# Attention without mask matmuls and with half-tile output work, and shorter lookups in the expert ranking, in a one-core encoder layer

## The reference

```python
s = einsum('bqhd,bkhd->bhqk', qb, k) * DA_DK ** -0.5       # 2 streams of 8 heads, 64 wide
mask = kchunk[None, :] <= (qpos // CHUNK)[:, None]         # chunks of 64 tokens
p = softmax(where(mask, s, -inf)).reshape(b, 8, 2, nq, nk)
a = p[:, :, 0] - lam * p[:, :, 1]
o = einsum('bhqk,bkhd->bqhd', a, v)                        # then normed per head and merged
...
t1, i1 = top_k(s1, 16); t2, i2 = top_k(s2, 16)             # PEER: per token and head
ts, ci = top_k(t1[:, None] + t2[None, :], 16)              # 16 best of the 256 sums
e = i1[ci // 16] * 128 + i2[ci % 16]                       # look up the two ranks' places
```

## Time and profile before

| | us |
|---|---|
| three runs | 2456.37, 2452.95, 2452.42 (median 2452.95) |
| the profiled execution | 2453.18 |
| its span, first to last instruction | 2451.4 |
| busy in the span: PE, DVE, ACT, POOL | 2297.4, 1542.0, 666.7, 1169.1 |
| attention and ranking within it | about 482 to 727, and about 998 to 1328 |

### The profile page before, as it was taken

How to read it: one execution, slowest core, us unless ns; L and a number is a source line. 1 busy time by engine, 2 the same in 40 slices (tenths; PEclk the granted TensorE clock), 3 DMA queues, 4 the chain that set the end, 5 groups by cost and what they waited for, 6 DMA issues and landing times.

```text
span 2451.4 us, 29790 instructions
## 1 busy us (share of the span) xinstructions
PE 2297.4 (94%) x11005; PEld 1758.7 (72%) x11005; DVE 1542.0 (63%) x2697; ACT 666.7 (27%) x1421; POOL 1169.1 (48%) x744
## 2 busy tenths in 40 slices
PE   6999999989979999998998999999799999999996
PEld 5899977755557987998998999999544444444442
DVE  3376654454553033699999999999455555555555
ACT  2334420133331122233343544444100100001011
POOL 8754555400003404426665777777344544445441
PEclk9999999955679999999999999999899999999998
DMA  6423233210031303226555999999999999999994
GB/s 232 149 95 107 97 106 120 99 47 18 17 116 55 131 30 130 78 89 219 171 176 149 352 355 359 360 370 346 327 359 380 376 386 374 373 382 383 379 382 167
DMA packets 220195, 541.96 MB, mean 221 GB/s; under 512 B 20129, under 2 KB 119266, under 8 KB 211106
## 3 DMA queue, kind: packets, MB, share of 16 engines
q1 hardware_dynamic: 113024, 243.30, 29.3%
q0 software_dynamic: 55424, 201.42, 21.6%
q10 hardware_dynamic: 51618, 95.52, 10.8%
HBM read 472.18 MB, written 67.67 MB: 220 GB/s over the span
## 4 chain that ended last, share of the span: by engine, by line
PE 56%; DVE 31%; issue 5%; DMA 4%; ACT 2%; SPq 2%; POOL 1%; ACTq 0%; POOLq 0%; DVEq 0%
PE ps L975 24%; PE ps L601 17%; DVE ring_u L1903 5%; PE ps L719 5%; DVE ps L1912 3%; PE ps L752 3%; DMA ge<-ge_scratch 3%; DVE hot L2059 2%; DVE hot L2057 2%; PE ps L580 2%; PE ps L802 2%; PE ps L756 1%; SPq L450 1%; DVE pickp L1983 1%; POOL wL L495 1%
## 5 line engine op out<-in xcount | busy, mean ns | idle before, releaser
L975 PE MATMUL ps<-vraw,gf 128*128 128x512 f32 x1536 | 665.7, 596 | 23.6 <-DVE gf L2073 14.5
L975 PEld LDWEIGHTS ps<-vraw,gf 128*128 128x128 f32 x1536 | 293.1, 191 | 395.6 <-issue 373.6
L510 POOL DMA_INDIRECT ring_u<-u_rows,place_of x192 | 234.4, 1221 | 414.2 <-DVE ring_u L1903 393.8
L491 POOL TENSOR_SCALAR wH<-raw 128x1024 fp32r<-128x1024 f32 x112 | 122.6, 1113 | 627.1 <-PE ps L601 475.7
L501 POOL TENSOR_TENSOR uL<-uraw,uH 128x1024 fp32r<-128x1024 f32 x128 | 323.3, 2539 | 116.6 <-ACT uH L1415 115.6
L927 PE MATMUL ps<-actH,uH 128*128 128x384 f32 x1024 | 347.9, 340 | 7.7 <-POOL uL L501 7.0
L927 PE MATMUL ps<-actL,uH 128*128 128x384 f32 x1024 | 343.6, 336 | 0.0
L927 PE MATMUL ps<-actH,uL 128*128 128x384 f32 x1024 | 343.4, 335 | 0.0
L1903 DVE SCALAR_TENSOR_TENSOR ring_u<-ring_u,xn 128x1024 f32<-128x1024 f32 x192 | 312.7, 1629 | 0.0
L601 PE MATMUL ps<-actH,wH 128*128 128x288 f32 (+1 forms) x960 | 287.4, 299 | 9.2 <-DVE actL L1573 9.2
L601 PE MATMUL ps<-actL,wH 128*128 128x288 f32 (+1 forms) x960 | 285.2, 297 | 0.0
(11 more groups left out here) (293 smaller groups left out, 3422.3 us busy)
## 6 DMA issues: line engine op xcount, KB each, us to landing
uraw<-wu SPq DMA_DIRECT2D x128, 512.0 KB, 4.6
vraw<-wv SPq DMA_DIRECT2D x128, 512.0 KB, 7.4
raw<-wts SPq DMA_DIRECT2D x56, 1024.0 KB, 4.9
ge_scratch<-ge ACTq DMA_DIRECT2D x128, 192.0 KB, 4.6
c_scratch<-cst ACTq DMA_DIRECT2D x12, 2048.0 KB, 10.1
cg<-c_scratch SPq DMA_DIRECT2D x32, 768.0 KB, 12.8
ge<-ge_scratch SPq DMA_DIRECT2D x128, 192.0 KB, 8.3
xres<-x ACTq DMA_DIRECT2D x2, 2048.0 KB, 11.9
```

Of the source, the lines that this page charges most:

```text
L491: pool.tensor_scalar(hi[:, cut], w[:, cut], 1.0, 1.0, ALU.mult, ALU.mult).then_inc(high_done, 1)
L510: pool.indirect_dma_start(out=ring_u[:, s % RING, :], out_offset=None, in_=a["u_rows"], in_offset=bass.IndirectOffsetOnAxis(ap=place_of[:, ...
L975: mm = pe.matmul(bank(2 * i + half), gf[:, q % GF_RING, i * P:(i + 1) * P], vraw[:, q % V_RING, half * CHUNK:(half + 1) * CHUNK], start=q ...
```

## The change

- No mask matmuls, no mask tensor and no load of it; each score matmul closes its own group.
- `maxima` takes two reductions, one over the first n-64 keys for all rows and one over the last 64 keys for rows 64 to 127 alone, and then the smaller of the two (negated) results for these rows. `exps` takes two activations per stream, split the same way, each with its own sum; the excluded block of the matrix is set to zero once at the start, and `combine` first adds the two sums (`zb` stays zero in the upper rows).
- In tiles 0 to 3 PE issues `scores` two units ahead, and DVE takes `maxima(u)` ahead of `combine(u-1)`. Tile 4 keeps the old order.
- Outputs are copied, normed, turned and merged by half tile (four heads, one PSUM bank), spread over the following eight units; `merge` is cut into `scale_outputs` and `merge`; the loads come by half tile too.
- In `rank`, the winner at place t of 16 can only have a rank below 4 for t < 4 and below 8 for t < 8, so the three lookups go over 4*4 + 4*8 + 8*16 = 176 instead of 256 elements per head and half, each cut into three instructions.

```diff
-                    mm = pe.matmul(bank(b, n), qT[half, h, t], kT[half, h, 0:n], start=True, stop=False)
+                    mm = pe.matmul(bank(b, n), qT[half, h, t], kT[half, h, 0:n], start=True, stop=True)
-                    mm = pe.matmul(ps[:, b * BANK + n - DK:b * BANK + n], mask[0:1, 0:P], mask[0:1, P:P + DK],
-                                   start=False, stop=True)
...
-            if h == 0 and i > 0:
-                pe.wait_ge(turned_used, i)
+            if h % 4 == 0 and i > 0:
+                pe.wait_ge(turned_used, 2 * i + h // 4 - 1)
...
         scores(0)
+        scores(1)
         for u, (i, h) in enumerate(UNITS):
-            if u + 1 < len(UNITS):
+            if u + 2 < pairs:
+                scores(u + 2)
+            elif pairs <= u + 1 < len(UNITS):
                 scores(u + 1)
             turn_probs(u)
-            if h == 1 and i > 0:
-                turn_outputs(i - 1)
+            if h % 4 == 3 and u > 3:
+                turn_outputs((u - 3) // 4 - 1)
...
+                    act.activation(prob[:, u % 2, s, 0:n - DK], bank(b, n - DK), ACT.Exp,
+                                   bias=sm["nmax"][:, col:col + 1], accum_out=sm["z"][:, col:col + 1])
+                    ins = act.activation(prob[DK:P, u % 2, s, n - DK:n], ps[DK:P, b * BANK + n - DK:b * BANK + n],
+                                         ACT.Exp, bias=sm["nmax"][DK:P, col:col + 1],
+                                         accum_out=sm["zb"][DK:P, col:col + 1])
...
+            j = (u - 4) // 4
+            if j >= 0 and h % 4 == 1:
+                copy_outputs(j)
+            if j >= 0 and h % 4 == 2:
+                root(j)
+            if j >= 1 and h % 4 == 1:
+                merged_high(j - 1)
+            if j >= 2 and h % 4 == 1:
+                act.wait_ge(ml_done, j - 1)
+                load_merge(j)
...
+                ve.tensor_reduce(nmax, src[:, :, 0:n - DK], AX, ALU.max, negate=True)
+                step.done(ve.tensor_reduce(sm["nm"][DK:P, :], src[DK:P, :, n - DK:n], AX, ALU.max, negate=True))
+                ve.tensor_tensor(nmax[DK:P], nmax[DK:P], sm["nm"][DK:P, :], ALU.min).then_inc(nm_ready, 1)
...
+                step.done(ve.tensor_tensor(rz, z, sm["zb"][:, 2 * (u % 2):2 * (u % 2) + 2], ALU.add))
...
+        ve.wait_ge(sc_ready, 1)
+        step.done(ve.memset(sm["zb"], 0.0))
+        for b in range(2):
+            ins = ve.memset(prob[0:DK, b].rearrange("p s (i k) -> p s i k", k=P)[:, :, :, DK:P], 0.0)
         for u, (i, h) in enumerate(UNITS):
-            if u > 0:
+            if i == TILES - 1:
                 combine(u - 1)
             maxima(u)
+            if u > 0 and i < TILES - 1:
+                combine(u - 1)
+            j = (u - 4) // 4
+            if j >= 0 and h % 4 == 2:
+                variance(j)
+            if j >= 0 and h % 4 == 3:
+                scale_outputs(j)
+            if j >= 1 and h % 4 == 0:
+                merge(j - 1)
+            if j >= 1 and h % 4 == 2:
+                merged_low(j - 1)
...
+            parts = [(slice(0, 4), 4), (slice(4, 8), 8), (slice(8, TOPK), TOPK)]
             for half in range(2):
-                step.done(ve.tensor_tensor(flat, ..., ALU.is_equal))
-                step.done(ve.tensor_tensor(hit, hit, ..., ALU.mult))
-                step.done(ve.tensor_reduce(chosen[0:rows, at, half, mine], flat, AX, ALU.add))
+                for ts, w in parts:
+                    ins = ve.tensor_tensor(hit[:, :, ts, 0:w], ..., ALU.is_equal)
+                step.done(ins)
+                for ts, w in parts:
+                    ins = ve.tensor_tensor(hit[:, :, ts, 0:w], hit[:, :, ts, 0:w], ..., ALU.mult)
+                step.done(ins)
+                for ts, w in parts:
+                    ins = ve.tensor_reduce(out[:, :, ts], hit[:, :, ts, 0:w], AX, ALU.add)
+                step.done(ins)
```

More of the change, by code:

```diff
@@ L1297, in _ @@
         load_x()
-        copy_outputs(last)
-        root(last)
+        merged_high(2 * last)
+        copy_outputs(2 * last + 1)
+        root(2 * last + 1)
         next_gain(2, MT + TILES)
-        merged_high(last)
-        act.wait_ge(ml_done, TILES)
+        merged_high(2 * last + 1)
+        act.wait_ge(ml_done, 2 * TILES)
         def norm_behind(variances):
@@ L1754, in _ @@
         osq = gain
[L1756 to L1776, removed]
-                part = sat[:, 4 * m:4 * m + 4, 0:rows]
-                ins = ve.scalar_tensor_tensor(part, bank(6 + m, 4 * rows).rearrange("p (k t) -> p k t", k=4),
-                                              sm["gsub"], part, ALU.mult, ALU.mult)
-            ins.then_inc(turned_used, 1)
-            ve.wait_ge(turned_used, i + 1)
-            ve.tensor_tensor(sat[:, :, 0:rows], sat[:, :, 0:rows], rt[:, :, 0:rows], ALU.add).then_inc(merged, 1)
@@ L1784, in merged_low, with variance @@
-        def merged_low(i):
+        def variance(j):
+            rows, cols = ROWS[j // 2], slice(j % 2 * CHUNK, (j % 2 + 1) * CHUNK)
+            oss, orstd = (sm[name][0:rows, 4 * (j % 2):4 * (j % 2) + 4] for name in ("oss", "orstd"))
+            ve.wait_ge(osb_ready, j + 1)
+            step.done(ve.tensor_tensor(osq[0:rows, cols], osb[0:rows, cols], osb[0:rows, cols], ALU.mult))
+            step.done(ve.tensor_reduce(oss, osq[0:rows, cols].rearrange("p (h d) -> p h d", h=4), AX, ALU.add))
+            ve.tensor_scalar(orstd, oss, 1.0 / DV, SUBLN_EPS, ALU.mult, ALU.add).then_inc(ovar_ready, 1)
@@ new lines, in scale_outputs, with merge @@
+        def scale_outputs(j):
+            rows = ROWS[j // 2]
+            orstd = sm["orstd"][0:rows, 4 * (j % 2):4 * (j % 2) + 4]
+            ve.wait_ge(ostd_ready, j + 1)
+            step.done(ve.reciprocal(orstd, orstd))
+            heads = osb[0:rows, j % 2 * CHUNK:(j % 2 + 1) * CHUNK].rearrange("p (h d) -> p h d", h=4)
+            ve.tensor_tensor(heads, heads, orstd.unsqueeze(2).broadcast_to([rows, 4, DV]), ALU.mult).then_inc(on_ready, 1)
+        def merge(j):
+            rows, heads = ROWS[j // 2], slice(4 * (j % 2), 4 * (j % 2) + 4)
+            ve.wait_ge(yt_ready, j + 1)
+            ve.wait_ge(sat_in, 32 * min(max(j + 1, 2) + (j == 2 * TILES - 2), 2 * TILES))
+            part = sat[:, heads, 0:rows]
+            ve.scalar_tensor_tensor(part, bank(6 + j % 2, 4 * rows).rearrange("p (k t) -> p k t", k=4),
+                                    sm["gsub"], part, ALU.mult, ALU.mult).then_inc(turned_used, 1)
+            ve.wait_ge(turned_used, j + 1)
+            ve.tensor_tensor(part, part, rt[:, heads, 0:rows], ALU.add).then_inc(merged, 1)
@@ L1806, in project_and_norm @@
+            if j >= 1 and h % 4 == 2:
+                merged_low(j - 1)
+        last = 2 * TILES - 1
+        combine(len(UNITS) - 1)
+        merge(last - 1)
+        merged_low(last - 1)
+        variance(last)
+        scale_outputs(last)
+        merge(last)
+        merged_low(last)
         def project_and_norm(n, variances):
```

141 lines of the change are left out of this document (67 added, 74 removed).

## The result

The changed kernel takes 2388.86 us (median of four runs, 2385.29 to 2391.82), against 2454.64 us for the kernel before in the same runs: a ratio of 0.9734, 95% interval 0.9719 to 0.9748. The forecast was 2400 us. The profiled execution of after took 2389.49 us, with a span of 2387.7 us, 63.7 us less than the span before.

A forecast was written before the change was run, and what follows sets the result against it. PE at the half clock was taken to bound attention's tiles 0 to 2, a three-step loop its full-clock part, and DVE ranking. Attention -46 and ranking -7 made -53 from 2453.2: 2400 us, range 2380 to 2421.

The forecast's parts named there:

- ranking: Ranking stage: shorter lookups give -4.8 us in full ranks and -2.2 in pair ranks, -7 in all, between -19 and +14.
- PE's work per unit: Attention tiles 1 to 3 without masks: 4.0, 5.5 and 7.1 us of PE per unit at the half clock.
- The clock: PE's clock in attention: half in tile 1, rising within tile 2, full for three quarters of tile 3.
- Rival 1: Attention: clock stays at 0.50 through tile 3; -37 us, 2416 us; chance 0.25.
- rival 3: Attention: clock is full from tile 1 on, leaving DVE's work; -62 us, 2391 us; chance 0.15.
- DVE's work: Attention: 4.0, 4.5 and 4.9 us of DVE per unit in tiles 1, 2 and 3, waits included.
- the wait of the merge: Attention: DVE stands at `merge` while PE turns outputs, some 1.6 us per half tile, 0.4 per unit.
- +0.6 us per unit: ACT in attention: two more activations a unit add about 0.6 us, and ACT is not the bound.
- Tile 0 and tile 4: Attention's first and last tiles: -5 us in tile 0; 0 in tile 4, with 3 us to either side.
- The rival that the loop of latencies stays: Attention: reordering fails; maximum, exponentials and combination stay in sequence; -24 us, 2429 us; chance 0.07.
- the 2.1 us wait: Full-rank halves: a two-operand DVE instruction waits for POOL; it may go (-2.1 us) or come twice (+2.1).
- rival 4: Ranking: 88 added two-operand DVE instructions may wait for POOL, up to 2.4 us each; 2503 us with 40 waits; chance 0.04.

The follow-up runs named there:

- the kernel with one maximum: After with one maximum over all keys of the row instead of the split one, against after (2388.86 us): 2383.96 us, ratio 0.9712.

## Why the prediction was right, and where it was not

**The time.** 2388.86 us lies in the range and 11 us below the forecast of 2400: attention gave 60 us where 46 were forecast, ranking 4.6 where 7 were.

**The term that was mis-sized: PE's work per unit.** The prediction priced the score pair without masks as twice the row of one stream, 2 x 1.58 us in tile 2, and so came to 4.0, 5.5 and 7.1 us per unit at the half clock. Measured in its place: 1.22 us (64x256) and 1.65 us (64x384) for both streams, so about 1.65 + 0.83 + 1.28 + 0.25 = 4.0 us in tile 2, below DVE's 4.5. With that, tile 2 took 35.2 instead of 40 us. In tile 1 the error was hidden by luck: PE's 4.0 us, really 1.22 + 0.62 + 0.85 + 0.25 = 2.9, happened to equal DVE's 4.0. The rows of before could not show the overlap, because the masks stood between all pairs; but the kernel puts each pair on different rows of the array, and what that allows was not asked.

**The clock.** By the table's intervals the mean clock of after was 0.50, 0.65 and 0.85 in tiles 1, 2 and 3. That is close to what the forecast took: half in tile 1, rising within tile 2, full for three quarters of tile 3. Rival 1 (0.50 throughout, 2416 us) and rival 3 (full from tile 1, 2391 us) are both off in the clock, yet the time is nearly that of rival 3: with the measured pair, PE at the half clock has about 4.0 us of work per unit in tile 2, less than DVE, so by this sum a full clock was not needed for DVE to set the pace. What the clock was worth apart from that no run shows.

**DVE's work.** Per unit tile 1 took 32.5 / 8 = 4.1 us for the 4.0 of the sum, tile 2 35.2 / 8 = 4.4 for 4.5, and tile 3 44.7 / 9 = 5.0 for 4.9. (The 44 us forecast for tile 3 hit by accident: they came from eight units with a share of PE at the half clock.) The reductions (1.09 and 0.30), the small instruction (0.16) and the sum (0.16) are close to their estimates, and the wait of the merge, 1.20 here and up to 1.7, to its 1.6. So DVE's time per unit was the part of the sum that held. It holds as a whole, gaps and waits included: the busy time alone is 3.3, 3.7 and 4.3 us per unit.

**ACT.** +0.6 us per unit was too little: each small exponential takes 309 ns and 186 more to read its sum, 2 x 0.5 = 1.0 us per unit, less 0.1 for the 64 columns that each large one loses (groups of ACT in after, columns as in rows 6):

```profile
L1228 ACT ACTIVATE prob<-ps,small 64x64 f32<-64x64 f32 x64 | 19.8, 309 | 0.8
...
L1228 ACT ACTIVATION_READ_ACCUMULATOR prob<-ps,small 64x1 f32 x64 | 11.9, 186 | 0.0
```

ACT is not the bound, as forecast, but so close that about half of DVE's next saving is lost, as the kernel with one maximum shows.

**Tile 0 and tile 4.** -9 and -5 us for -5 and 0. Tile 0's interval is shorter by a unit through the new order, so seven units at 22.4 / 7 = 3.2 us stand against eight at 3.9; tile 4's gain comes from the half tiles, which the prediction had put at nothing there, with 3 us to either side.

**Order and half tiles.** The rival that the loop of latencies stays was priced at 2429 us; after with the old order took 2413. That the parts don't add is plain from the runs: without masks 56, half tiles 27, new lookups 6 us one at a time, together 66. What the half tiles are worth inside the change was not run apart.

**Ranking.** 4.6 for 7. Per full-rank half the lookups save 1.4 us (53.8 to 45.2 us in six halves), more than the 0.8 taken, with the 2.1 us wait neither gone nor doubled; the pair ranks save 3.0 us; and 7 us come back in other instructions, a place in which the prediction didn't look. PE's wait fell by 4.1 us, so the gain went through. The lock of rival 4 did not grow beyond that.

## What to carry to other kernels

Before a small matmul is removed, see what it stands between: two matmuls on different rows of the array can share their time, and a depth-1 matmul between them took that away. Its place cost 43 us here, and the same matmuls behind the pair only 13. Price a step by what its neighbours could do without it, not only by its own rows. When the bound leaves one engine, look at the next two at once: here DVE and ACT were so close that half of DVE's next saving was lost.

## What the runs showed of the hardware

- Two f32 matmuls of 64 rows each, on rows 0 to 63 and 64 to 127, take the time of one: 1.65 us for 64x384 at the half clock (one alone 1.64 to 1.65), 0.92 to 1.13 us at the full clock for 64x384 and 64x512 (one 64x512 alone 1.12, in before).
- A depth-1 matmul on row 0 shared its time with neither: 40 us for 64 of them between the pairs, 8 us behind.
- PE busy without a gap for 92 us at 1.2 GHz (496 to 588, before with half tiles) and then at 2.4 GHz; in after, 2.4 GHz comes and goes in stretches of a few us while PE has gaps.
